# The gate-half bias of each expert: from two products on TensorE to a copy by ScalarE

## The reference

```
hu = xblk @ w_up_gate[e] + b_up_gate[e]      # 1024 -> 2048
g, u = hu[:, :1024], hu[:, 1024:]            # gate half, up half
g = minimum(g, 7);  u = clip(u, -7, 7)
act = g * sigmoid(1.702 * g) * (u + 1)
y = act @ w_down[e] + b_down[e]
```

## Time and profile before

| | |
|---|---|
| median of 3 runs | 1755.31 us (1753.12 to 1757.16) |
| span of the profiled execution | 1751.3 us, 26655 instructions |
| its own time | not given apart; the median is 4.0 us above its span |
| PE busy | 1724.3 us (98%) |
| PE weight loads | 1275.0 us (73%) |
| DVE busy | 1441.9 us (82%) |
| ACT busy | 1140.3 us (65%) |
| POOL busy | 518.5 us (30%) |
| chain that ended last | PE 92%, DVE 4%, DMA 1%, ACT 1% |
| HBM | 479.17 MB read, 24.39 MB written |

### The profile page before, as it was taken

One profiled execution on the slowest core, in us unless ns is written; L12 is line 12 of the kernel. 1 busy time (PEld: TensorE's weight loads), 2 busy tenths in 40 slices (PEclk: granted clock), 3 DMA queues, 4 the chain that ended last, 5 costly groups with the idle time before them and its releaser, 6 DMA issues.

```text
span 1751.3 us, 26655 instructions
## 1 busy us (share of the span) xinstructions
PE 1724.3 (98%) x8893; PEld 1275.0 (73%) x8893; DVE 1441.9 (82%) x1489; ACT 1140.3 (65%) x1126; POOL 518.5 (30%) x293
## 2 busy tenths in 40 slices
PE   8999999999999999999999999999999999999997
PEld 7778777777777867677777777777777777777765
DVE  4666676567655889999998999899989998999898
ACT  4544564455454577778777777777777777777783
POOL 1102201210220144223553354334423442344340
PEclk9999999999999999999999999999999999999998
DMA  7431333133125589999999999999999999999985
GB/s 212 145 97 56 88 108 96 48 108 96 48 97 224 189 342 390 352 350 402 382 386 380 370 370 375 382 367 372 377 381 370 368 381 380 368 365 384 381 329 232
DMA packets 159188, 488.19 MB, mean 279 GB/s; under 512 B 13250, under 2 KB 83186, under 8 KB 125744
## 3 DMA queue, kind: packets, MB, share of 16 engines
q1 hardware_dynamic: 151248, 469.03, 72.6%
q0 software_dynamic: 7088, 16.52, 3.0%
q10 hardware_dynamic: 816, 2.19, 0.3%
HBM read 479.17 MB, written 24.39 MB: 288 GB/s over the span
## 4 chain that ended last, share of the span: by engine, by line
PE 92%; DVE 4%; DMA 1%; issue 1%; ACT 1%; DVEq 0%; SPq 0%; ACTq 0%
PE psum L333 27%; PE psum L335 27%; PE psum L334 27%; DVE wL L1756 2%; PE psum L714 1%; PE psum L744 1%; PE psum L1037 1%; PE psum L730 1%; PE psum L985 1%; DMA wraw<-in_w_up_gate 1%; PE psum L680 1%; PE psum L697 1%; PE psum L1001 1%; PE psum L778 0%; ACT wH L432 0%
## 5 line engine op out<-in xcount | busy, mean ns | idle before, releaser
L1756 DVE TENSOR_TENSOR wL<-wraw,wH 128x2048 fp32r<-128x2048 f32 x388 | 880.9, 2293 | 85.1 <-ACT wH L432 84.4
L432 ACT ACTIVATE wH<-wraw 128x2048 fp32r<-128x2048 f32 x388 | 744.5, 1920 | 278.6 <-PE psum L335 264.9
L333 PE MATMUL psum<-wH,xTH 128*96 128x512 f32 x1040 | 416.4, 400 | 2.0 <-DVE wL L1756 1.1
L335 PE MATMUL psum<-wH,xTL 128*96 128x512 f32 x1040 | 408.7, 393 | 0.0
L334 PE MATMUL psum<-wL,xTH 128*96 128x512 f32 x1040 | 408.1, 392 | 0.0
L2203 POOL PARTITION_BROADCAST cst<-brow x64 | 276.3, 4318 | 267.7 <-DMA xg<-x2d,ixg 218.3
L333 PEld LDWEIGHTS psum<-wH,xTH 128*96 128x96 f32 x1040 | 167.9, 161 | 74.7 <-DVE wL L1756 2.6
L335 PEld LDWEIGHTS psum<-wH,xTL 128*96 128x96 f32 x1040 | 167.8, 161 | 72.4
L334 PEld LDWEIGHTS psum<-wL,xTH 128*96 128x96 f32 x1040 | 168.0, 162 | 69.4
L333 PE MATMUL psum<-wH,aTH 128*96 128x512 f32 x496 | 197.0, 397 | 0.0
L335 PE MATMUL psum<-wH,aTL 128*96 128x512 f32 x496 | 195.4, 394 | 0.0
(11 more groups left out here) (273 smaller groups left out, 2264.2 us busy)
## 6 DMA issues: line engine op xcount, KB each, us to landing
wraw<-in_w_up_gate SPq DMA_DIRECT2D x256, 1024.0 KB, 8.2
wraw<-in_w_down SPq DMA_DIRECT2D x128, 1024.0 KB, 7.3
fraw<-in_w_in SPq DMA_DIRECT2D x68, 512.0 KB, 4.1
yd<-in_consts SPq DMA_DIRECT2D x8, 1024.0 KB, 8.0
wraw<-yd SPq DMA_DIRECT2D x3, 2048.0 KB, 9.6
wraw<-in_w_out SPq DMA_DIRECT2D x4, 1024.0 KB
xt<-in_x SPq DMA_DIRECT2D x4, 512.0 KB, 5.5
hres<-in_x SPq DMA_DIRECT2D x4, 512.0 KB, 5.1
```

Source lines behind the costliest of these rows:

```text
L333: nc.tensor.matmul(ps, lh, rh, start=start, stop=False)
L335: return nc.tensor.matmul(ps, ll, rh, start=False, stop=stop)
L432: nc.scalar.activation(wH[:, b % SPLIT, :], raw(b), ACT.Copy).then_inc(p_hi, 1)
L1756: V.tensor_tensor(wL[:, b % SPLIT, :], raw(b), wH[:, b % SPLIT, :].bitcast(F32), ALU.subtract).then_inc(p_lo, 1)
```

## The change

Every expert's gate-half bias row is loaded by SP into 96 partitions (`load_gate_bias`, a broadcast of one row of 4 KB into `bias_g`), once the copy of the row before has been made. ACT copies it from there into banks 0 and 1 (`seed`), after `x_high` and ahead of the next weight pieces. The products of banks 0 and 1 then all accumulate (start=False), and `up_part` waits for the seed. So that banks 0 and 1 accumulate on what ACT has written, TensorE runs one product over each of them with start=True once, after the last logits (`mark`). The table `bias`, its three loads, its splitting, `sel` and `select` go. `brow` moves into a part of the constants' tile that is no longer read by then, and `b_step` counts the up half alone.

```diff
@@ SP: load_gate_bias, and where it is issued
-            sp.wait_ge(p_lo, 2)
-            for r in range(3):
-                sp.dma_start(braw[r * NE:(r + 1) * NE, :], b_up_gate[0, :, 0:FF]).then_inc(b_in, 16)
...
+            def load_gate_bias(i, e):
+
+                if not first(i):
+                    sp.wait_ge(seed_ready, i)
+                sp.dma_start(bias_g[0:BLK, :], b_up_gate[0][bass.ds(e, 1), 0:FF].to_broadcast([BLK, FF])).then_inc(bg_in, 16)
+
...
-            sp.wait_ge(b_step, BIAS_STEPS)
+            load_gate_bias(0, 0)
             load_bias_row(0, 0)
...
-            def load_body(e, begun=0):
+            def load_body(e, begun=0, last=False):
                 for p in range(begun, 8):
                     load_piece(e, p, up_src(e, p))
                     if p == 1:
                         load_bias_row(e, e)
                 for q in range(4):
+                    if q == 0 and not last:
+                        load_gate_bias(e + 1, e + 1)
                     load_piece(e, 8 + q, down_src(e - 1, q))
...
             load_piece(1, 0, up_src(1, 0))
+            load_gate_bias(1, 1)
             load_body(1, 1)
@@ TensorE
+            def mark():
+
+                for n in range(2):
+                    last = nc.tensor.matmul(bank[n], tri[:, 1, :], tri[:, :, :].rearrange("p a s -> p (a s)").unsqueeze(1).to_broadcast([P, 2, 2 * P]),
+                                            start=True, stop=True)
+                last.then_inc(marked, 1)
...
             logits(3)
+            mark()
             first_rows(2)
...
             def up_part(i, over=False, turn_last=False):
...
-                if not first(i):
-                    pe.wait_ge(ucl_ready, 2 * i - 1)
-                    pe.wait_ge(sg_ready, i)
-                pe.wait_ge(sel_ready, i + 1)
                 if first(i):
-                    pe.wait_ge(b_step, BIAS_STEPS)
-                    pe.wait_ge(rT_ready, 2 * NT)
                     pe.wait_ge(top_ready, NT)
                     pe.wait_ge(pos_free, 1)
-                for n in range(2):
-                    nc.tensor.matmul(bank[n][0:BLK, :], sel[:, 0:BLK], bias[:, n * 512:(n + 1) * 512], start=True, stop=False)
+                else:
+                    pe.wait_ge(ucl_ready, 2 * i - 1)
+                pe.wait_ge(seed_ready, i + 1)
@@ ScalarE
-            for n in range(3):
-                bias_high(n)
...
+            def seed(i):
+
+                act.wait_ge(bg_in, 16 * i + 16)
+                if first(i):
+                    act.wait_ge(marked, 1)
+                else:
+                    act.wait_ge(sg_ready, i)
+                A(hu[0:BLK, 0:FF], bias_g[0:BLK, :], ACT.Copy).then_inc(seed_ready, 1)
+
             high(act, 0, 7)
+            seed(0)
             first_high()
...
             silu(0)
             x_high(1, used(up_at(0), 8))
+            seed(1)
             high(act, 1, 1)
             high(act, 1, 2)
...
                 if prefetch:
                     x_high(i + 1, used((i, 0), 8))
+                    seed(i + 1)
                 high(act, i + 1, 0)
@@ VectorE, in body
                 clip_up(i)
-                if prefetch:
-                    select(i + 1)
                 low_piece(i, 11)
```

## The result

| | before | after |
|---|---|---|
| median, us (4 runs each) | 1754.78 (1753.12 to 1757.16) | 1788.71 (1786.09 to 1790.14) |
| ratio, 95% interval | | 1.019 (1.0177 to 1.0203) |
| span of the profiled execution, us | 1751.3 | 1788.4 (its time 1790.09) |
| PE busy | 98% | 96% |
| HBM read, MB | 479.17 | 491.34 |

The change costs 34 us where 10.4 were to be gained. The products did leave TensorE, and the copy costs ScalarE what was reckoned. What went wrong is the broadcast that feeds the copy: the transfers have become the bound.

A forecast was written before the change was run, and what follows sets the result against it. TensorE was taken to bound the expert stage. 12.0 - 0.5 - 0.43 - 0.9 + 0.2 = 10.4 us takes the span from 1751.3 to 1740.9; with 4.0 around it, 1744.9 us, range for 8 in 10 1741 to 1752.

The forecast's parts named there:

- What is added to the transfers: SP's queue, per expert: a 0.39 MB row to 96 partitions costs 0.96 us at 408 GB/s; TensorE stays the bound.
- The prediction's own turning point: Settled experts: a row holding the queue 35.01 - 32.3 = 2.7 us makes the transfers the bound.
- the dear end: Row's price if it runs like the gather at 243 GB/s: 1.4 us beyond the bytes, in all 2.4 us.
- rival (d): Settled experts: transfers become the bound, row 3.4 us, 35.7 us per expert, 21 us more, 1776 us; chance 0.08.
- Rival (e): All transfers held to 376 GB/s: 36.1 us per expert, 32 us more, 1787 us; chance 0.01.
- The first seed: Before the experts: falls into the 5.69 us in which ScalarE waits before 593.75 us, so costs nothing.
- Where the queue was behind: After 767 us, expert 6 and following: later landings make TensorE wait, cost 0.9 us, between 0 and 1.9.
- The pair's 0.43 us: TensorE's two bias products, removed per expert: 0.43 us each, 28 pairs on the path, 12.0 us gained.
- The seed: ScalarE's copy of 96x1024 f32 to PSUM per expert: 1.05 us, between xTH and a weight copy, hidden.
- Expert 1: No down half covers the seed there, so VectorE starts late: cost 0.5 us, 0 to 1.4.
- The marking products: Two TensorE products of 128x512 bf16 after the last logits, before the experts: cost 0.43 us.
- The sum of 10.4 us: Whole kernel: 12.0 - 0.5 - 0.43 - 0.9 + 0.2 = 10.4 us gained, 8.0 to 12.3 with the terms' ends.

The follow-up runs named there:

- experiment 3: Changed kernel with the gate row of experts 2 to 31 sent to 128 partitions instead of 96; 1748.32 us, ratio 0.9967.
- experiment 6: Version of experiment 8 with the gate row of experts 2 to 31 sent as two transfers of 64 partitions; 1827.92 us, ratio 1.0403.
- experiment 7: Changed kernel with the gate row of experts 2 to 31 sent to 16 partitions instead of 96; 1747.42 us, ratio 0.9963.
- experiment 8: Changed kernel with all gate rows sent to 128 partitions, the first one loaded after the first two x2d writes landed; 1745.77 us, ratio 0.9948.

## Why the prediction was wrong

**The step that failed** is in "What is added to the transfers": "The price 0.96 us (0.39 MB at 408) assumes that a row sent to many partitions runs like others." It did not. With the 32.3 us of the earlier trace rows as what the other transfers of an expert need, the periods give the price of the row:

| rows of 4 KB | MB | period, us | price, us |
|---|---|---|---|
| 1 | 0.004 | 34.57 | at most 2.3 |
| 16 | 0.07 | 34.55 | at most 2.3 |
| 64 | 0.26 | 36.09 | 3.8 |
| 96 | 0.39 | 35.95 | 3.6 |
| 96, different | 0.39 | 36.17 | 3.9 |
| 112 | 0.46 | 36.48 | 4.2 |
| 128 | 0.52 | 34.57 | at most 2.3 |
| 64 + 64 | 0.52 | 37.58 | 5.3 |

At 34.57 and 34.55 TensorE is the bound, so those rows give a limit only. The prices lean on one stretch of the kernel before, two landings 32.3 us apart. The prediction's own turning point was 2.7 us; 3.6 lies beyond it and the sign turned. The comparison was at fault: of two rows at hand I took as "the same kind of transfer" the norm's gain, which went to 128 partitions, and set aside the gather, 96 rows wide, whose 243 GB/s gave 2.4 us. What decided was the partition count (of 64 and up), not whether a row is repeated. Even the dear end was too low, so the range would have missed by either row; rival (d), at 3.4 us and 35.7 us per expert, was the mechanism that came, and got 0.08; its 1776 us is 13 short, as the price, the first clip and the experts after it all cost more. Rival (e), at 1787, is nearest in number by luck: its reason, all transfers held to 376 GB/s, does not hold, since in experiment 3 the queue moved 395 GB/s over the settled stage, against 377 in the changed kernel. The lines are those of experiment 3 and of the changed kernel:

```profile
900.00:1600.00 700.00, 699.90 (x3238) 495.91 (x3237) 651.53 (x387) 544.06 (x387) 280.47 (x123) 1.00 1.01 395
900.00:1600.00 700.00, 679.64 (x3117) 475.99 (x3116) 629.89 (x369) 524.16 (x371) 309.87 (x119) 1.00 1.01 377
```

**Why the count decides** is open. What is shown is that equal bytes on equal partitions cost 3.0 us more in two transfers of 64 rows (experiment 6), and that beside a row to 64, 96 or 112 partitions the packets of the weight pieces slow down, and beside one to 128 they do not (experiment 3). The Trainium skill, page "DMA: Bandwidth & Descriptors", section "The descriptor swizzle", says that in a transfer to 128 partitions each of the 16 DMA engines writes eight partitions that hang on one port of SBUF; by its formula partitions 0 to 15 fall to four engines, not to the two that the expectation of experiment 7 has. The section "Why a DMA increments its semaphore by 16 and not by 1" of that page of the Trainium skill says that a 96-partition tile also goes to 16 engines; worked out from that, an estimate, each has six rows. If these follow one another, engines write to partitions of each other's ports while their neighbours are at the weight pieces, which would slow those as well. The slowing is what the packets here show; its reason is an inference, since no trace here names the engine of a packet. The Trainium skill, page "SBUF — State Buffer", section "Door 1: The DMA port swizzle (why `[64,N]` ≈ `[32,N]`)", puts partitions 0 to 63 on half the ports with 218 GB/s at most; worked out from that, an estimate, 0.26 MB take 1.2 us. Here they cost 3.8 in a full queue, so that rule has the direction (0.64 us by the bytes at 408 GB/s) but not the size.

**The first row's transfer was left out.** The first seed was costed at nothing, and its transfer not at all. It went out on SP's queue ahead of two up pieces and before the writes of x2d, which ScalarE's queue issues and on whose landing VectorE's next scaled tile waits (2.9 us in the changed kernel, 0.4 before); 3.3 us of the 7.0 at the first clip lie here and in what follows, the rest being that execution's own. The granted clock of the changed kernel fell behind that, at 585.4 us, after TensorE had stood idle for 1.21 us up to 582.96. This is the stretch (0.50 is the 1.2 GHz level), in which products start 0.43 us apart instead of 0.23:

```profile
585.40:588.80 3.40, 3.40 (x10) 2.66 (x9) 2.42 (x10) 0.00 (x0) 0.00 (x0) 0.50 1.03 423
```

**Where the queue was behind** (priced at 0.9 us), the two periods from expert 4 to expert 6 cost 8.0 in the changed kernel (41.2 and 36.5 us between the first clips, before 36.4 and 33.3) and 5.5 in the version with 128 rows (40.4 and 34.8); with one partition they cost nothing (36.3 and 33.0). The transfers meet a slow stretch there that was in the kernel before as well. Kernel before:

```profile
748.00:757.00 9.00, 9.00 (x46) 6.46 (x45) 8.97 (x7) 6.15 (x6) 2.66 (x2) 1.00 1.03 147
```

Experiment 8:

```profile
748.00:760.00 12.00, 12.00 (x59) 8.56 (x58) 8.86 (x6) 5.20 (x4) 2.66 (x2) 1.00 1.06 161
```

As I read it, a queue with pieces in reserve rides over it, and one that is just fast enough passes all of it on; no run takes the reserve apart from the rest. I had priced one transfer's delay there, not the loss of the reserve.

**What held.** The pair's 0.43 us: 35.01 - 34.57 = 0.44. The seed: 1.05 reckoned, 1.03 measured, hidden between the experts. Expert 1: 0.5 reckoned; in experiment 8 VectorE waits there for the weight copy behind the seed:

```profile
624.17 4.96 DVE L1741 TENSOR_TENSOR wL<-wraw,wH 128x2048 fp32r<-128x2048 f32 x2 [0.55 <-ACT wH L401]
```

The marking products: 0.43 us in two starts (595.50 and 595.93 us). The first seed itself: TensorE waits 1.7 us for it in the changed kernel, and waited 1.5 us for `sel` at that place before. The sum of 10.4 us can be set against experiment 8, whose span is 7.3 us under that of before. There the seventh clip comes 5.7 us later than before (829.7 against 824.0), 5.5 of it from the two periods above, and all the gain lies behind it:

```profile
L1953 DVE SCALAR_TENSOR_TENSOR ucl<-psum,cst x7: 1210/1214/1220, 619.6 to 829.7; 96x1024 f32<-96x1024 f32 x7
L1953 DVE SCALAR_TENSOR_TENSOR ucl<-psum,cst x25: 1207/1214/1216, 829.7 to 1658.7; 96x1024 f32<-96x1024 f32 x25
```

829.0 us for 24 experts against 840.3: 11.3 us, where 24 x 0.43 = 10.3 were expected. Another 1.7 us come behind the last of these clips, where the granted clock of the kernel before fell from 1706.4 to 1709.8 us and that of experiment 8 did not. So the term for TensorE held, and the whole came near by setting this against a loss that was reckoned too small. The 4.0 us taken for what lies around a span was too much: in the runs that list both it is 1.7 to 2.2, and of the times of the kernel before only 1753.12, not the median, lies that near its span of 1751.3.

## What to carry to other kernels

Where a transfer queue is nearly full, price an added transfer by a row with the same number of partitions, not by one of the same kind, and then ask what is left in reserve. Where it goes to many partitions, try all 128, in one transfer: here 0.13 MB per expert that nobody reads saved 40 us. A load that is needed late also has a place in the queue; look at what queues behind it, the writes of other engines too.

## What the runs showed of the hardware

- Broadcasts of one 4 KB row cost, in a queue otherwise full, 3.6 to 4.2 us for 64, 96 or 112 partitions and at most 2.3 us for 1, 16 or 128; two of 64 cost 5.3.
- The slowing reaches the pieces around: 296 GB/s over 7 us for 0.39 MB of broadcast, and 8 KB packets of 0.40 us in place of 0.31.
- Products that accumulate (start=False) on values that ScalarE has written to PSUM add to them (experiment 8 gives the reference's result so). One product with start=True over each of those banks ahead of the first expert was enough for all 32.
- The queue moved 395 GB/s from 900 to 1600 us in experiment 3, and 377 in the changed kernel, with the DMA share at 1.01 in both: a full share does not say at what rate.
